# PEER's value stage: the first block of every pair of up-units as six products of 128 columns

## The reference, cut to what matters

```python
def peer_ffn(h, w_query, sub_keys, expert_u, expert_v):
    q = (ht @ w_query).reshape(T, Hh, 2, PEER_HALF)
    scores = jnp.einsum('thpd,hpkd->thpk', q, sub_keys)
    s_top, i_top = lax.top_k(scores, K)
    ...
    best, pos = lax.top_k(cand, K)
    expert_idx = jnp.take_along_axis(cand_idx, pos, axis=-1)
    gates = jax.nn.softmax(best, axis=-1)

    def block(args):
        xb, idx, g = args
        u = expert_u[idx]
        a = jax.nn.gelu(jnp.einsum('tkd,td->tk', u, xb)) * g
        return jnp.einsum('tk,tkd->td', a, expert_v[idx])
```

## Time and profile before

| | us |
|---|---|
| median of 3 runs | 3076.28 (3075.04 to 3084.94) |
| the profiled execution's own time | 3079.91 |
| its span, first to last instruction | 3078.1 |
| TensorE busy in the span | 3023.9 |
| VectorE, ScalarE, GpSimd busy | 2184.3, 1611.1, 266.6 |
| mean granted TensorE clock, as a share | 0.994 |

### The profile page before, as it was taken

How to read it: one execution, slowest core, us unless ns; L and a number is a source line. 1 busy time by engine, 2 the same in 40 slices (tenths; PEclk the granted TensorE clock), 3 DMA queues, 4 the chain that set the end, 5 groups by cost and what they waited for, 6 DMA issues and landing times.

```text
span 3078.1 us, 53282 instructions
## 1 busy us (share of the span) xinstructions
PE 3023.9 (98%) x22540; PEld 2851.7 (93%) x22540; DVE 2184.3 (71%) x3454; ACT 1611.1 (52%) x2390; POOL 266.6 (9%) x249
## 2 busy tenths in 40 slices
PE   8999999999999999999999999999999999999999
PEld 8998999999899998999999998879999999999887
DVE  5877887876788746899555557675669975555676
ACT  5575544565544455556544445556445554444444
POOL 0010001000101001830000000000156000000000
PEclk9999999999999999999999999999999999999999
DMA  6772577775267544457866657655444687666663
GB/s 230 268 250 96 205 252 253 266 268 194 97 248 282 179 154 172 157 179 286 290 218 218 215 201 244 210 182 187 165 168 175 233 298 238 218 218 218 220 232 123
DMA packets 153260, 654.59 MB, mean 213 GB/s; under 512 B 10332, under 2 KB 77472, under 8 KB 78272
## 3 DMA queue, kind: packets, MB, share of 16 engines
q1 hardware_dynamic: 96576, 584.09, 53.3%
q10 hardware_dynamic: 56032, 65.66, 6.4%
q0 software_dynamic: 416, 1.45, 0.2%
HBM read 616.55 MB, written 34.61 MB: 212 GB/s over the span
## 4 chain that ended last, share of the span: by engine, by line
PE 88%; DVE 8%; ACT 2%; issue 1%; DMA 1%; POOL 0%; ACTq 0%; DVEq 0%
PE ps L596 19%; PE ps L598 19%; PE ps L597 19%; PE ps L601 8%; PE ps L602 8%; PE ps L603 8%; DVE w_lo L1544 2%; PE ps L1025 2%; PE ps L764 2%; ACT w_hi L1094 1%; DVE raw L1539 0%; DVE h_lo L1562 0%; PE ps L996 0%; DVE at L2034 0%; DVE at L2024 0%
## 5 line engine op out<-in xcount | busy, mean ns | idle before, releaser
L1544 DVE TENSOR_TENSOR w_lo<-raw,w_hi 128x1024 fp32r<-128x1024 f32 x932 | 1137.7, 1227 | 597.8 <-ACT w_hi L1094 596.7
L1094 ACT ACTIVATE w_hi<-raw 128x1024 fp32r<-128x1024 f32 x1000 | 1050.6, 1055 | 679.7 <-PE ps L598 429.2
L596 PE MATMUL ps<-h_hi,w_hi 128*128 128x256 f32 x4224 | 1186.2, 281 | 7.3 <-DVE w_lo L1544 6.1
L597 PE MATMUL ps<-h_lo,w_hi 128*128 128x256 f32 x4224 | 1177.0, 279 | 0.0
L598 PE MATMUL ps<-h_hi,w_lo 128*128 128x256 f32 x4224 | 1176.8, 279 | 0.0
L596 PEld LDWEIGHTS ps<-h_hi,w_hi 128*128 128x128 f32 x4224 | 794.1, 188 | 13.5 <-issue 6.2
L598 PEld LDWEIGHTS ps<-h_hi,w_lo 128*128 128x128 f32 x4224 | 799.9, 189 | 0.0
L597 PEld LDWEIGHTS ps<-h_lo,w_hi 128*128 128x128 f32 x4224 | 795.0, 188 | 2.8 <-issue 0.2
L601 PE MATMUL ps<-w_hi,at 128*128 128x512 f32 x1024 | 398.5, 389 | 3.1 <-DVE at L2083 3.1
L602 PE MATMUL ps<-w_lo,at 128*128 128x512 f32 x1024 | 398.3, 389 | 0.0
L603 PE MATMUL ps<-w_hi,at 128*128 128x512 f32 x1024 | 398.3, 389 | 0.0
(11 more groups left out here) (281 smaller groups left out, 3259.1 us busy)
## 6 DMA issues: line engine op xcount, KB each, us to landing
raw<-in_peer_u SPq DMA_DIRECT2D x128, 1024.0 KB, 4.8
raw<-in_peer_v SPq DMA_DIRECT2D x128, 1024.0 KB, 4.8
raw<-in_ffn_gu SPq DMA_DIRECT2D x88, 1024.0 KB, 4.9
raw<-in_ada_w SPq DMA_DIRECT2D x48, 1024.0 KB, 5.2
raw<-in_ffn_down SPq DMA_DIRECT2D x44, 1024.0 KB, 4.9
gates<-at ACTq DMA_DIRECT2D x32, 1024.0 KB, 4.6
at<-gates ACTq DMA_DIRECT2D x24, 1024.0 KB, 5.9
raw<-in_w_in SPq DMA_DIRECT2D x16, 1024.0 KB, 4.8
```

What stands on the lines that cost most here:

```text
L596: e.matmul(o, lhs[0], rhs[0], start=start, stop=False)
L597: e.matmul(o, lhs[0], rhs[1], start=False, stop=False)
L1094: e.activation(whi[:, u % NPAIR, :], raw(k, half), ACT.Copy).then_inc(hi_done.hit(u), 1)
L1544: e.tensor_tensor(wlo[:, m % NPAIR, :], raw(k, half), whi[:, m % NPAIR, :].bitcast(FP), ALU.subtract).then_inc(w_lo_dve.hit(m), 1)
```

## The change

In the value stage, for the first unit of each up-pair (even u, from 66 up), the first of the 8 blocks is computed as two triples of 128 columns, one for each half of the tokens, and the other seven blocks stay triples of 256 columns. These units go through `loose`. The second unit of a pair, and all pairs before the value stage, are as before.

```diff
-            def project(q, n, o):
+            def project(q, n, o, parted=False):
                 wh, wl = weights(n)
                 for k in range(KT):
                     c = slice(k * 128, (k + 1) * 128)
                     w.wait_ge(h_lo, h_lo(q, k))
+                    if parted and k == 0:
+                        for tt in range(2):
+                            z = slice(tt * 128, (tt + 1) * 128)
+                            loose(o[:, z], (wh[:, c], wl[:, c]), h_part(k, z), tt == 0, False)
+                        continue
+                    if parted:
+                        t = loose(o, (wh[:, c], wl[:, c]), h_part(k), False, k == KT - 1)
+                        continue
                     t = triple(o, (wh[:, c], wl[:, c]), h_part(k), k == 0, k == KT - 1)
                 t.then_inc(used.hit(n), 1)
...
-                    project(q, unit[("peer_u", l), u], u_bank[0][:, u % 2 * T:(u % 2 + 1) * T])
+                    project(q, unit[("peer_u", l), u], u_bank[0][:, u % 2 * T:(u % 2 + 1) * T], u % 2 == 0 and u >= 2 * NPAIRS)
```

## The result

The changed kernel takes 3107.85 us (3103.76 to 3110.75, 4 runs) against 3078.62 us (3075.04 to 3084.94, 4 runs) of the kernel before: a ratio of 1.0076, 95% interval 1.0058 to 1.0094, or +23.4 us. The forecast was +0.25%, within the 0.3% that I called no change; the measured +0.76% lies beyond it, where rival 1 stood. Taken by the ratio the time is 3078.62 x 1.0076 = 3102, inside the range of 3078 to 3104; the median itself lies 4 us above its end. The profiled execution has a span of 3106.1 us against 3078.1.

A forecast was written before the change was run, and what follows sets the result against it. TensorE, a gapless line of products in the value stages, was taken as the bound. Per pair 0.672 + 5.103 = 5.775 us against 5.65, +0.125; 62 pairs give +7.8 us on 3076.28: 3084 us, range 3078 to 3104.

The forecast's parts named there:

- rival 1: Value stage, behind the six narrow products: the 45 keep the long step, 0.1177 us each; +19.8 us, 3096; chance 0.30.
- The count: Value stages: 62 pairs, three products of 256 columns become six of 128 in each; 186 more matmul records.
- the cover: Value stages: ScalarE's and VectorE's weight splitting has slack, busy 48% and 56%; the one wait of 1.5 us stays.
- the clock: TensorE's granted clock is 1.00 and the change leaves no gap; a fall was a rival given nothing of its own.
- The price of a narrow product: First block of a pair: six 128-column products are load-bound, 0.112 us each, +0.319 us a pair.
- Rivals 2 and 3: Narrow products: loads hidden, 3079 or 3067 us (chances 0.04, 0.05); or run as plain float32, 3138 or 3126 (0.12).
- The step of the 45 behind them: 256-column products behind the six narrow ones in a pair: short step, 45 x 0.1134 = 5.103 us.
- the other dearer cases: Value-stage pairs partly short and partly long, 3087 to 3094, chance 0.07; narrow products as plain float32, 0.12.
- The likeliest single case: Value-stage pairs with load-bound narrow products and the short step behind: +7.8 us, 3084 us, chance 0.40.
- The 512-column products: 24 value products behind each pair: 5.44 us, 0.2267 each; a step other than 0.227 would break the prediction's frame.
- The border of 9.2 us: Whole kernel: 0.3%, the least difference a measurement can tell; passed once 8 of 62 pairs stay long.

The follow-up runs named there:

- e2: Changed kernel with the first block of each pair as four groups of 64 columns, 12 products: 3138.9 us (kernel before beside it 3089.7).
- f2: Changed kernel with the six-product split moved to the second block of the pair: 3097.1 us (kernel before beside it 3083.8).
- f4: Changed kernel with the first two blocks of the pair split, 12 products of 128 columns: 3103.8 us (kernel before beside it 3083.8).
- h2: Changed kernel with the last value product ahead of each pair halved into two of 256 columns: 3090.2 us (kernel before beside it 3082.2).
- g1: Changed kernel without the split, still through `loose`; last value product ahead of a pair as two of 256 columns: 3078.8 us (kernel before 3085.8).
- h1: Kernel before with only the last value product ahead of each pair as two of 256 columns: 3073.23 us, ratio 0.9966.
- e4: Changed kernel with only the first product of the first block split in two of 128 columns: 3079.4 us (kernel before beside it 3089.7).
- f3: Changed kernel without the split; one tiny float16 product issued just before the pair's first product: 3095.7 us (kernel before beside it 3083.8).

## Why the prediction was right and wrong

**The count, the cover and the clock** were right: 186 more records, 62 pairs, TensorE busy throughout, no new wait, clock 1.00.

**The price of a narrow product** was right. I took 0.112 each and +0.319 a pair with the long step; the trace has loads 0.11 apart and 5.97 - 5.65 = +0.32 (0.315). e2 shows that the columns do not set it: 64 cost as much as 128. Rivals 2 and 3 are out: 0.11 is neither the 0.065 of the float16 row nor two records of it. The Trainium skill's page "TensorE: Matmul & The Clock Gate", section "Back-to-back issue gap", has some 81 ns per product at 128 columns; the trace does not agree for these 4-byte operands, with 0.111 us.

**The step of the 45 behind them** is the step of the working that failed. I took the short one, "the commoner sequel to blocks of 128 columns", 45 x 0.1134 = 5.10 us. It is the long one in all 62 pairs, 5.30 us, and rival 1 came true with its price, 19.8 us. This is 12.0 of the 14.5 us by which 7.8 fell short of 22.3.

The rows that I counted could not carry the choice. The first stretch of rows 5, which stood for the long step, has 1615 products in the same 183 us in f2 and 1613 in f4, which is the short step; the stretches behind L996, which stood for the short one, are long in f2 and f3. None of this code was touched: the sequel to an interlude that I had read off one execution comes out the other way in another. Nor does the sequel follow from the number of narrow products alone (2 and 12 short, 4 and 6 long). h2 against the changed kernel speaks for the way in which the stream enters the group, but h2 is a single execution, so that it fell into the short step by chance is not ruled out; g1 and h1, with the same halved product, had it too.

The range held the ratio's 3102 because it reached up to rival 1, and the chance of 0.60 on slower came from it and the other dearer cases. The likeliest single case was wrong and gave a third of the change.

**The 512-column products** were taken as fixed at 5.44 us; that was the frame I said could fail, and it did, by a little. Their first steps in the changed kernel:

```profile
1567.02 0.40 PE L602 MATMUL ps<-w_lo,at 128*128 128x512 f32 x1
1567.26 0.40 PE L603 MATMUL ps<-w_hi,at 128*128 128x512 f32 x1
1567.49 0.39 PE L601 MATMUL ps<-w_hi,at 128*128 128x512 f32 x1
...
1568.41 0.40 PE L602 MATMUL ps<-w_lo,at 128*128 128x512 f32 x1
1568.64 0.39 PE L603 MATMUL ps<-w_hi,at 128*128 128x512 f32 x1
1568.88 0.39 PE L601 MATMUL ps<-w_hi,at 128*128 128x512 f32 x1
```

Eight steps from 1567.02 to 1568.88 take 0.2325 each, against 0.2267 before; behind them the block runs at 0.2267 again. The block's 0.045, times 62, is 2.8 us and is the rest: 19.5 + 2.8 = 22.3. Why the first steps are longer there, and by 0.015 in all behind the short step (e2, e4, f4), no run shows.

**The border of 9.2 us** was crossed as rival 1 said it would be, with far more than its 8 pairs.

## What to carry to other kernels

Before a product of these 4-byte operands is made narrower than 256 columns, look at the distance of its weight loads. Here it is 0.111 us when nothing hides it: 256 columns do (0.1133), 128 and 64 do not, and a width between was not run. So splitting a product of 256 columns costs nearly a full load, while splitting one of 512 into two of 256 is all but free. The stream of 256-column products ran at two steps 4% apart without any gap in the profile. Compare the step of the same line in different stretches and in several executions before a forecast leans on it; and where it is long, a cheap change at its entry is worth a try, measured over many executions. And read such a change from the stretch that it touches, since the rest of the kernel may move by as much from one execution to the next.

## What the runs showed that I had not expected

- The same 256-column products took 0.1133 us in the value stages of h1 and 0.1177 in those of the kernel before, in every pair of the profile; in other stretches the step differs between executions (883 and 852 products in the same 100 us). The short step is not there from the first product: in h1 the first steps of a pair are 0.121, 0.122, 0.115 and 0.115 and then 0.1133, in h2 it comes from the sixth wide product on, and in the changed kernel it does not come. What distinguishes the two steps, and which entry leads to which, stays open: no run here shows it, and I could not say beforehand which of the kernels would get which.
- Products of 512 columns take a little longer too behind some entries: blocks of 5.440, 5.455 and 5.485 us. The extra lies in the first three steps (0.231 to 0.233 in e4) or the first nine (0.225 to 0.236 in the changed kernel); the others are 0.2267.
- A float16 product of a single column between products of the other type costs some 0.3 us, nearly three of the 0.111 steps. The sum: f3 is 0.114 us a pair above the kernel before, though the short step behind it gives 0.2 back. How much of it comes from the other type and how much from the shape was not tried.
